# Hybrid encoder layer on one core: state recurrence started before the within-chunk sums, residual rows loaded tile by tile, the fifth turn of the projection moved forward

## The reference, cut to what matters

```
h = h + 1/2 * SwiGLU(RMSNorm(h))
n = RMSNorm(h); z = n @ W_in        # z -> c_q | c_kv | k_rope | u | g_attn | g_ssm
attn = MLA(c_q, c_kv, k_rope)
y    = S5_forward(u) + S5_backward(u) + D*u        # complex diagonal recurrence, 32 groups of 16
ssm  = GLU(GELU(y))
h = h + (sig(g_attn)*attn@W_oa + sig(g_ssm)*ssm@W_os) @ W_out
h = h + 1/2 * SwiGLU(RMSNorm(h));  out = RMSNorm(h)
```

## Time and profile before

| | before |
|---|---|
| median of 3 runs | 2278.45 us |
| range of the 3 runs | 2277.05 to 2278.88 us |
| the profiled execution, its own time | 2281.39 us |
| its span, first to last instruction | 2279.3 us |
| PE busy | 2150.0 us, 94% |
| DVE busy | 1468.7 us, 64% |
| ACT busy | 918.1 us, 40% |
| POOL busy | 611.4 us, 27% |
| DMA | 263.00 MB, mean 115 GB/s |

### The profile page before, as it was taken

How to read it: one execution, slowest core, us unless ns; L and a number is a source line. 1 busy time by engine, 2 the same in 40 slices (tenths; PEclk the granted TensorE clock), 3 DMA queues, 4 the chain that set the end, 5 groups by cost and what they waited for, 6 DMA issues and landing times. The chain is left out here.

```text
span 2279.3 us, 27668 instructions
## 1 busy us (share of the span) xinstructions
PE 2150.0 (94%) x10074; PEld 1778.2 (78%) x10074; DVE 1468.7 (64%) x2300; ACT 918.1 (40%) x1551; POOL 611.4 (27%) x510
## 2 busy tenths in 40 slices
PE   5899999999998999959899999889899999999997
PEld 4778888887887998848777887778678888887886
DVE  7787667657777426951457887554766565657777
ACT  5423333324445342124426778422532323224444
POOL 5336877740000021201002333100533333310000
PEclk9999999999998999979999999999999999999999
DMA  3423334349333455311430000273123232349333
GB/s 120 107 89 122 118 117 139 122 171 339 97 112 114 135 86 163 97 42 55 131 130 25 7 6 15 93 257 126 56 88 120 88 121 88 120 148 342 101 97 111
DMA packets 234471, 263.00 MB, mean 115 GB/s; under 512 B 34720, under 2 KB 169376, under 8 KB 233824
## 3 DMA queue, kind: packets, MB, share of 16 engines
q1 hardware_dynamic: 234336, 261.23, 36.1%
HBM read 184.60 MB, written 76.58 MB: 115 GB/s over the span
## 5 line engine op out<-in xcount | busy, mean ns | idle before, releaser
L48 PE MATMUL psum<-f_B_hi,f_A_hi 128*128 128x512 f32 x1232 | 488.4, 396 | 24.7 <-DVE f_A_lo L1053 12.9
L50 PE MATMUL psum<-f_B_hi,f_A_lo 128*128 128x512 f32 x1232 | 483.3, 392 | 0.0
L49 PE MATMUL psum<-f_B_lo,f_A_hi 128*128 128x512 f32 x1232 | 483.0, 392 | 0.0
L48 PEld LDWEIGHTS psum<-f_B_hi,f_A_hi 128*128 128x128 f32 x1232 | 233.5, 190 | 76.5 <-DVE f_A_lo L1053 20.1
L50 PEld LDWEIGHTS psum<-f_B_hi,f_A_lo 128*128 128x128 f32 x1232 | 233.3, 189 | 49.4
L49 PEld LDWEIGHTS psum<-f_B_lo,f_A_hi 128*128 128x128 f32 x1232 | 233.6, 190 | 47.6
L939 ACT CAST f_A_hi<-f_S 128x512 fp32r<-128x512 f32 x176 | 109.3, 622 | 348.4 <-PE psum L50 340.3
L48 PE MATMUL psum<-f_wd,f_hh 128*128 128x512 f32 x616 | 240.4, 390 | 3.6 <-DVE f_wd L1099 3.6
L50 PE MATMUL psum<-f_wd,f_hh 128*128 128x512 f32 x616 | 240.4, 390 | 0.0
L49 PE MATMUL psum<-f_wd,f_hh 128*128 128x512 f32 x616 | 240.3, 390 | 0.0
L1328 POOL TENSOR_TENSOR f_S<-f_raw 128x512 f32<-128x512 f32 x86 | 129.9, 1511 | 304.4 <-DVE f_A_lo L1053 284.2
(11 more groups left out here) (335 smaller groups left out, 4191.7 us busy)
## 6 DMA issues: line engine op xcount, KB each, us to landing
f_h_raw<-hidden SPq DMA_DIRECT2D x154, 256.0 KB, 2.6
hidden<-rows SPq DMA_DIRECT2D x44, 768.0 KB, 4.7
f_raw<-ffn_w_gate SPq DMA_DIRECT2D x44, 512.0 KB, 5.2
f_raw<-ffn_w_up SPq DMA_DIRECT2D x44, 512.0 KB, 5.0
f_wd_raw<-ffn_w_down SPq DMA_DIRECT2D x44, 512.0 KB, 8.9
rows<-x SPq DMA_DIRECT2D x16, 512.0 KB, 7.4
ga_raw<-w_in SPq DMA_DIRECT2D x16, 512.0 KB, 4.6
gates<-ga_sig SPq DMA_DIRECT2D x32, 256.0 KB, 2.3
```

Of the source, the lines that this page charges most:

```text
L48: pe.matmul(out, lhs_hi, rhs_hi, start=first, stop=False, skip_group_check=go_on)
L49: pe.matmul(out, lhs_hi, rhs_lo, start=False, stop=False, skip_group_check=go_on)
L50: return pe.matmul(out, lhs_lo, rhs_hi, start=False, stop=last, skip_group_check=go_on)
```

## The change

In the projection, turn 4 stands ahead of unit 0, one turn follows each of the units 0 to 2, and the order on ACT and DVE follows that. In the ssm phase the DVE recurrence starts as soon as ss_H is whole, and the eight within-chunk adds stand behind its steps 10 to 13 and 28 to 31; PE does gate product 1 between within-chunk q = 3 and q = 4 and no longer waits for the adds before gate product 2; lam8 is loaded second; ACT's two forward copies stand behind the sigmoid of product 11. In the merge the residual rows come in eight loads of 512 KB, four at n = 4 to 7 and four at units 7 to 10.

```diff
@@ Norm.act / Norm.dve
-        for n in range(2):
-            rp.high(act, n)
         for i in range(self.AHEAD, ST):
+            rp.high(act, i - self.AHEAD)
             self.act_high(act, i)
-            if i < ST - 2:
-                rp.high(act, i - 2)
...
-        rp.low(dve, 0)
-        self.dve_rows(dve, 5)
-        rp.low(dve, 1)
         for i in range(self.AHEAD, ST):
+            rp.low(dve, i - self.AHEAD)
+            if i + 1 < ST:
+                self.dve_rows(dve, i + 1)
             self.dve_low(dve, i)
-            if i < ST - 2:
-                self.dve_rows(dve, i + 2)
-                rp.low(dve, i - 2)
@@ project_phase, tensor
-            for i in range(norm.AHEAD):
+            for i in range(norm.AHEAD + 1):
                 norm.pe(pe, i)
...
-                for i in ((4,), (5,), (6, 7), ())[n]:
-                    norm.pe(pe, i)
+                if norm.AHEAD + 1 + n < ST:
+                    norm.pe(pe, norm.AHEAD + 1 + n)
@@ ssm_phase
+WITHIN_AFTER = (10, 11, 12, 13, 28, 29, 30, 31)
...
             side.gp.load(sp, 0)
+            sp.dma_start(lam8[:].rearrange("p a b g -> p (a b g)"), lam8_dram).then_inc(s["lam"], 16)
...
             side.gp.load(sp, 1)
-            sp.dma_start(lam8[:].rearrange("p a b g -> p (a b g)"), lam8_dram).then_inc(s["lam"], 16)
...
             for q in range(NQ):
+                if q == NQ // 2:
+                    side.gp.product(pe, 1)
...
                 mm.then_inc(s["within"], 1)
+            for n in range(2, GATES_FIRST):
+                side.gp.product(pe, n)
             pe.wait_ge(s["wadd"], NQ)
-            for n in range(1, GATES_FIRST):
-                side.gp.product(pe, n)
...
-                if n == GATES_FIRST - 5:
+                if n == GATES_FIRST - 2:
                     forward(0)
                     forward(1)
...
-            for q in range(NQ):
+            def within(q):
...
                 dve.tensor_tensor(H[:, n + 1], H[:, n + 1], prod[:, 1, ::-1], ALU.add).then_inc(s["scan"], 1)
+                if n in WITHIN_AFTER:
+                    within(WITHIN_AFTER.index(n))
@@ merge_phase
+        def take(sp, m):
+            sp.dma_start(rows[:, m, :], kept[m * P:(m + 1) * P, :]).then_inc(s_kept[m // QUAD], 16)
...
-                if n == 1:
-                    sp.dma_start(rows[:], kept.rearrange("(m p) d -> p m d", p=P)).then_inc(s_kept, 16)
+                if n >= QUAD:
+                    take(sp, n - QUAD)
...
                 load(sp, u)
+                if KT - 1 <= u < KT + 3:
+                    take(sp, u - KT + 1 + QUAD)
...
-                    dve.wait_ge(s_kept, 16)
+                    dve.wait_ge(s_kept[0], 16 * QUAD)
...
+            dve.wait_ge(s_kept[1], 16 * QUAD)
```

More of the change, by code:

```diff
@@ L2427, in merge_phase @@
         s_g, s_p = [sem("g0"), sem("g1")], [sem("p0"), sem("p1")]
-        s_sum, s_hi, s_lo, s_kept = sem("sum"), sem("hi"), sem("lo"), sem("kept")
+        s_sum, s_hi, s_lo, s_kept = sem("sum"), sem("hi"), sem("lo"), [sem("kept0"), sem("kept1")]
         NU = 2 * KT
```

## The result

| | before | changed |
|---|---|---|
| median (4 runs each, same chip) | 2277.84 us | 2249.26 us |
| range | 2277.05 to 2278.88 | 2247.07 to 2251.64 |
| ratio | | 0.9874, 95% interval 0.9857 to 0.9892 |
| profiled execution, own time | 2281.39 us | 2250.36 us |
| its span | 2279.3 us | 2248.3 us |

Faster by 28.6 us in the medians and by 31.0 in the two spans. The forecast was 2250.3, a gain of 28.2.

What follows compares the result with a forecast made beforehand. PE, busy 94%, was taken to set the end; gains of 2.2 (projection), 15.3 (ssm gates) and 10.7 (merge), 28.2 us in all, take 2281.39 to 2253.2, or a median of 2250.3; range 2243 to 2259.

Steps and rivals of the forecast that it cites:

- The three places: PE stands still, then runs at half clock: projection 4.67 us, ssm gates 23.40 us, merge 7.73 us.
- the new wait: PE before gate product 3: C_mat issued 11.0 us later, at 884.1, sigmoid store 0 queued behind it; 9.2 us.
- the seam: Projection start: turn 4 goes into PE's 4.67 us wait and later waiting goes; 2.2 us gained, bounds 0.8 to 4.2.
- the merge: Merge phase: gate tile 2 no longer queues behind 4 MB of residual rows; 10.7 us gained (7.73 + 2.9), bounds 7 to 10.7.
- The place of the copies: Ssm gates: forward copies behind sigmoid 11 remove PE's 23.4 us wait and 2.6 us of slow clock.
- Rival 1: Ssm gates: the wait before product 3 does not reach PE, store or C_mat being quicker; gain 40, 2238.5 us; chance 0.10.
- The slow clock behind the wait: Gate product 3 runs partly at half clock after PE's wait before it; 2.6 to 2.9 us, 2.6 taken.
- The recurrence: Ssm phase, DVE: starts 858.3 instead of 873.80, ends 994.7, off the path by some 14 us; early start buys nothing itself.
- Rival 3: Ssm phase: the recurrence becomes the bound, eating the whole 28 us gain if it ends at 1044; example 2285; chance 0.02.
- Rival 2: Merge: small 512 KB loads cannot keep 412 GB/s; gain 7 instead of 10.7, 2254 us; chance 0.12.
- the prediction's own signs of being wrong: PE waiting before product 2 or between q, a forward copy awaiting DVE, L2539 awaiting DMA in merge, slow units 0 to 3.

## Why the prediction was right

The total: 2250.3 forecast, 2249.26 and 2249.14 measured. The three places, and the new wait that the change makes, came where they were forecast. That the total is within 1.1 us is in part luck: the seam is worth 2.6 or 4.2 from one execution to the next and the merge 8.9 to 10.8, and the untouched code behind the outputs scatters by 2 to 3.4. Step by step:

**The seam** was put at 2.2; it is 2.6. All waiting went, as said (1.5 + 0.79 = 2.3). The other 0.3 is the clock: unit 0 went from 738.51 to 742.57, 4.06 us instead of 4.43, and in this stretch of the changed kernel the granted clock is 0.75 where it was 0.50. The prediction had bounded this by 4.2 and taken zero, "because unit 0 stood at half clock after a gap whose larger part stays". In this trace that is nearly so. In six of the nine traces with the new seam it is not: unit 0 took 2.5 us there, and the gain was the upper bound of 4.2.

```profile
738.00:740.00 2.00, 1.49 (x5) 1.42 (x6) 2.00 (x3) 0.29 (x1) 0.00 (x0) 0.75 1.05 350
```

**The place of the copies** was put at 23.4 + 2.6, 26.0 in all. Alone on the kernel before it gave 25.9 to the outputs and 26 in the medians.

**The new wait** was put at 9.2 us before product 3; it is 9.26, with C_mat at 881.95. Counted from the phase's start, which the prediction left where it was, that is 0.2 later than 884.1 less the 2.4 that the phase begins earlier. The transfer to POOL's low took 20.4 us against 20.46. Rival 1, the store passing C_mat, falls: 15.8 us again. The slow clock behind the wait was sized 2.6 from the 23.4 us wait; it was 1.8. Product 3 went from 902.40 to 1016.68 - 9 x 11.25 = 915.43, 13.03 us. In the other traces with the same code up to there the product took 1.4 to 2.3 us more than 11.25, so 2.6 was high in all of them. So the phase gained 16.05 and not 15.3. (By the prediction's own numbers, 1035.12 less 1019.7, its gain was 15.4.)

**The recurrence** was put at 858.3 to 994.7, 136.4 us; it ran from 856.04 to 990.68, 134.6 us. The start is the phase's 2.4 us. Eleven POOL lows lie inside it, as forecast; why it is 1.8 us shorter than the sum was not looked into. That its early start buys nothing by itself is shown by the late recurrence (0.8 us, inside the scatter). Rival 3, in which it becomes the bound, did not come true here. It is what happens in the kernel with the early store and a late recurrence, where the outputs wait 9.99 us.

**The merge** was put at 10.7 and is 10.8 between the two profiles. Undone, it cost 9.4 in the trace and 7.8 in the medians. The wait repeats (7.73, 7.14, and 7.05 in the run with the copies alone), what the clock adds does not: 2.9, 2.1 and 1.7 for the product behind it. Rival 2 fell as far as PE goes: behind the first gate tile DVE waited 0.44 and 1.23 us for two more, PE never. A wait of this multiplication for a DMA was one of the prediction's own signs of being wrong, and it came, too short to reach PE.

The timeline of DVE in the merge, changed kernel:

```profile
1449.61 1.22 DVE L2543 TENSOR_TENSOR mg_val<-psum,mg_gate 128x1024 f32<-128x1024 f32 x1 [10.21 <-DMA mg_gate<-gates]
...
1454.79 1.23 DVE L2543 TENSOR_TENSOR mg_val<-psum,mg_gate 128x1024 f32<-128x1024 f32 x1 [0.44 <-DMA mg_gate<-gates]
...
1458.97 1.22 DVE L2543 TENSOR_TENSOR mg_val<-psum,mg_gate 128x1024 f32<-128x1024 f32 x1
...
1468.55 1.22 DVE L2543 TENSOR_TENSOR mg_val<-psum,mg_gate 128x1024 f32<-128x1024 f32 x1 [1.23 <-DMA mg_gate<-gates]
```

Gate tile 2, the one that was 16.7 us on its way, is there when DVE comes to it at 1458.97. The 412 GB/s that the prediction held against this rival did not show what 512 KB loads reach, since the 4 MB load was under way too. (It also took 2.5 MB for 6.1 us and 1.75 MB for 4.2; at its own rate of 10.2 us for 4 MB they are 6.4 and 4.5, which changes nothing.) The changed kernel shows it: with no load above 512 KB, 397 GB/s between 1463 and 1480, and before, between 1473 and 1489 with the 4 MB among them, it was 397 as well. The Trainium skill, DMA: Bandwidth & Descriptors, section Bandwidth, asks for DMAs of 1 MiB or more to reach 75% of peak. Here the pieces of 512 KB cost no rate that these two stretches show, and taking the 4 MB apart was worth 8 to 11 us: what counted was who stood behind the load.

## What to carry to other kernels

When an in-order engine waits for a slow side computation, ask first where it has to ask for it: moving four copies three gate products down the list gave 26 us, while starting the computation sooner gave nothing by itself once that was done. Of every step that lets another one start later, follow the DMA that waits for it, and what queues behind that DMA: two stores of 256 KB behind a 4 MB load cost PE a wait of 9.3 us, and moving it ahead gave 11.7. When one load in a shared queue is not needed for a long time, cut it up and put the pieces behind what is needed now.

## What the runs showed that I had not expected

The cost of a wait in slow clock does not follow its length. Behind 23.40 us a product took 2.6 us longer, behind 9.26 it took 1.8, behind 7.73, 7.14 and 7.05 it took 2.9, 2.1 and 1.7. It does not repeat at one place either: behind the wait before product 3 (8.7 to 9.4 us) it was between 1.4 and 2.3. The same wait of 2.5 us in the mixer was followed by a half-clock stretch in the profile before and by none in the one after, 1.7 us of difference in code that no edit touched. Parts of 2 us can be read only from mark to mark within a trace, not from medians of four runs.

Less than the whole change is faster than the whole. The copies (26), the seam (2.6 to 4.2) and the merge (9 to 11) add up to 38 to 41 us, and together in one kernel they gave 37.3 in the medians. The changed kernel has 28.6, because its remaining parts, the early recurrence and the product between, cost it some 9 us in the medians. These three parts with the early store, and without the other two, were not tried, nor was an order in which the early recurrence gains something clear of the scatter.
